# In a mixture-of-experts loop, SyncE issues an expert's gate and up weight loads ahead of its wait for the previous expert's landing

## The reference

```python
def moe(h, p):                        # 64 experts, top 8, 1152 tokens, fp32
    ...
    order = jnp.argsort(flat_e)       # assignments sorted by expert, padded to blocks of 128
    ...
    def expert_block(args):
        xb, e = args                  # 128 x 1024, the block's expert
        return (jax.nn.silu(xb @ p["w_exp_gate"][e]) * (xb @ p["w_exp_up"][e])) @ p["w_exp_down"][e]
    ...
    shared = (jax.nn.silu(x @ p["w_sh_gate"]) * (x @ p["w_sh_up"])) @ p["w_sh_down"]
    return (routed + shared)
```

## Time and profile before

| | before |
|---|---|
| median of 3 runs | 1864.94 us (1858.88 to 1868.56) |
| the profiled execution | 1868.01 us, of which the span of the instructions is 1866.2 us |
| granted TensorE clock, mean over the span | 0.967 |
| PE busy | 1712.8 us (92%) |
| DVE, ACT, POOL busy | 929.8, 845.4, 766.8 us |
| data moved | 389.75 MB, mean 209 GB/s |
| routed part | about 745 to 1800 us, 104 blocks |

### The profile page before, as it was taken

The page is one execution under the profiler, slowest core; times in us unless marked ns, Lnnn a source line. Parts: engine busy times, 40 slices in busy tenths (PEclk is TensorE's granted clock), DMA queues, the critical chain, the costliest instruction groups (busy, mean ns, idle before and its releaser), DMA issues.

```text
span 1866.2 us, 32108 instructions
## 1 busy us (share of the span) xinstructions
PE 1712.8 (92%) x8570; PEld 1331.5 (71%) x8571; DVE 929.8 (50%) x1442; ACT 845.4 (45%) x950; POOL 766.8 (41%) x445
## 2 busy tenths in 40 slices
PE   6899999999899778999989989999999989999845
PEld 2677788888455656888877877888878767887621
DVE  7432210177478843564463555334644654465529
ACT  2320012441133512675565666445765765566622
POOL 3230000400004552565555556535665556646530
PEclk9999999998999888999999999999999999999978
DMA  8515521023442533697788889866987788778666
GB/s 343 179 55 179 171 91 37 15 91 122 171 170 91 195 88 138 227 336 233 216 309 260 251 295 332 245 164 187 330 302 223 258 289 286 223 251 281 230 226 265
DMA packets 102447, 389.75 MB, mean 209 GB/s; under 512 B 21916, under 2 KB 38553, under 8 KB 74624
## 3 DMA queue, kind: packets, MB, share of 16 engines
q1 hardware_dynamic: 62576, 289.25, 41.9%
q0 software_dynamic: 37232, 90.42, 19.2%
q10 hardware_dynamic: 2592, 9.44, 1.8%
HBM read 339.94 MB, written 84.72 MB: 228 GB/s over the span
## 4 chain that ended last, share of the span: by engine, by line
PE 62%; DMA 13%; DVE 8%; issue 6%; ACT 5%; POOL 3%; ACTq 2%; SPq 1%; POOLq 0%; DVEq 0%
PE ps L856 32%; PE ps L2001 12%; DMA arena<-hx_dram,arena 5%; DMA raw<-w_exp_up 4%; PE ps L911 4%; PE ps L2142 4%; POOL d_split L594 2%; DMA acc_dram<-arena 2%; PE ps L1924 2%; ACT d_split L658 1%; PE ps L2132 1%; PE ps L1974 1%; ACTq L440 1%; PE ps L888 1%; PE ps L2097 1%
## 5 line engine op out<-in xcount | busy, mean ns | idle before, releaser
L856 PE MATMUL ps<-gu_split,xT 128*128 (+1 forms) x2712 | 641.7, 392 | 6.6 <-issue 6.2
L856 PEld LDWEIGHTS ps<-gu_split,xT 128*128 128x128 f32 x2712 | 510.9, 189 | 119.0 <-issue 13.5
L856 PE MATMUL ps<-d_split,hTe 128*128 (+1 forms) x1356 | 351.1, 409 | 37.6 <-ACT arena L734 35.5
L594 POOL TENSOR_TENSOR d_split<-raw,d_split (+1 forms) x65 | 299.4, 4606 | 196.4 <-ACT d_split L658 195.8
L987 DVE TENSOR_TENSOR gu_split<-raw,gu_split (+1 forms) x130 | 294.6, 2308 | 141.0 <-ACT gu_split L653 137.3
L856 PEld LDWEIGHTS ps<-d_split,hTe 128*128 128x128 f32 x1356 | 254.7, 194 | 93.9 <-issue 43.8
L653 ACT ACTIVATE gu_split<-raw (+1 forms) x130 | 241.8, 1908 | 70.5 <-SPq L496 48.0
L613 POOL DMA_INDIRECT arena<-hx_dram,arena x108 | 139.8, 1295 | 189.1 <-DVE arena L1157 154.8
L622 POOL DMA_INDIRECT acc_dram<-arena x104 | 175.1, 1684 | 92.5 <-DVE arena L1162 58.2
L1151 DVE TENSOR_TENSOR arena<-ps,arena 128x256 f32<-128x256 f32 x113 | 70.5, 624 | 276.8 <-ACT arena L740 273.3
L1141 DVE TENSOR_TENSOR xT<-ps,xT 128x1024 fp32r<-128x1024 f32 x115 | 140.8, 1224 | 106.4 <-ACT xT L712 98.2
(11 more groups left out here) (284 smaller groups left out, 1436.8 us busy)
## 6 DMA issues: line engine op xcount, KB each, us to landing
raw<-w_exp_gate SPq DMA_DIRECT2D x64, 1024.0 KB
raw<-w_exp_up SPq DMA_DIRECT2D x64, 1024.0 KB
raw<-w_exp_down SPq DMA_DIRECT2D x64, 1024.0 KB
arena<-w_ada SPq DMA_DIRECT2D x16, 1024.0 KB, 4.9
arena<-x_dram SPq DMA_DIRECT2D x18, 512.0 KB, 10.4
arena<-acc_dram SPq DMA_DIRECT2D x18, 512.0 KB, 11.2
arena<-ada_halves SPq DMA_DIRECT2D x4, 2048.0 KB, 24.3
w_raw<-w_in SPq DMA_DIRECT2D x16, 512.0 KB, 4.9
```

The source lines that it names most:

```text
L594: tt(d_split(q, 1), raw_d(q), d_split(q, 0).bitcast(F32), ALU.subtract).then_inc(d_low, 1)
L856: last = mm(dst, lhs(a, j), rhs(b, j), start=(t == 0), stop=(t == len(terms) - 1))
```

## The change

In SP's loop, `publish_gu` of expert x-1 moves from ahead of the wait for x-2's slot to behind the two issues for expert x. Nothing else is touched; the number of instructions stays the same on all engines.

```diff
@@ -536,9 +536,9 @@
                 for q in range(2):
 
                     x = 2 * m + 1 + q
-                    publish_gu(q, m + 1)
                     sp.wait_ge(gu_low, x - 1)
                     load_gate_up(sp, 1 - q, row("gate", x - 1), row("up", x - 1))
+                    publish_gu(q, m + 1)
                     sp.wait_ge(d_low, x - 2)
                     load_down(sp, q, row("down", x - 2))
                     publish_d(1 - q, m + q)
```

## The result

The changed kernel takes 1876.25 us (median of 9 runs, 1868.49 to 1879.74), the kernel before beside it 1863.85 us (9 runs, 1857.98 to 1870.66). The ratio is 1.0070 with a 95% interval of 1.0052 to 1.0087: slower by 13 us, with 10 to 16 as bounds. The forecast was 1874 us, 9 us or 0.5% above, so it lies just under that.

What follows compares the result with a forecast made beforehand. Expert matmuls fill most of the chain; slow stretches are bound by a ring through ACT, POOL and SP. Lengthening it gives +9.8 us, sooner loads -1, so about +9 us on the 1864.94 median: 1874 us, range 1862 to 1884.

Steps and rivals of the forecast that it cites:

- Where SP stands in the chain: SP matters only in slow stretches of one-block experts, about 11.96 us per block against 9.26 where PE is full.
- four entries with 0.88 or 0.89 us: Time from SP's down issue to ACT's gate copy, read as the landing not being late there.
- third place: Four ring periods from 1475.43 to 1526.30 us, 50.87 together; forecast to lose 5.0 us.
- last place: Three ring periods from 1721.41 to 1759.73 us, 38.32 together; entry unchanged, forecast to lose 1.6 us.
- The ring: Loop of ACT's down copy, POOL's down split, SP's down issue and signal, ACT's gate copy; 12.54 us becomes 13.68.
- four places: Where one-block experts follow one another, from 956.90, 1089.59, 1475.43 and 1721.41 us; losses +1.5, +1.7, +5.0, +1.6, sum +9.8 us.
- The price of a signal, 1.14 us: Delay of SP's signal in the ring: 0.29 set-up, 0.80 two issues, 0.05 more set-up; bounds 0.80 and 1.3.
- The sum by place: Entry delay plus lengthened periods, new minus old, added over the ring's four places: +9.8 us.
- What the change gives back, -1 us: Loads starting sooner share less transfer time with gathers: 0 to one us at each place, -4 at most, -1 taken.
- Outside the ring nothing: Where PE is busy throughout, the later signal needs 1.45 us of 2.28 available, so it costs nothing.
- fourth rival: Margin outside the ring fails: about 13 places lose up to 1 us each, +10 to +20 us; chance 0.12.
- The rule on issue time: Skill page's rule would put the moved issues at nothing, sum -4 us; the forecast charged 0.80 us per signal instead.

Runs made afterwards that it cites:

- late signal alone: Against the kernel before, SP notes the landing ahead of the loads as before; only its signal to ACT moves behind the two issues; 1.0102, +19 us.
- SP out of POOL's wait: ACT issues and awaits the down loads instead of SP; against the kernel before, 0.9886 and 0.9884 in the changed order, 1.0006 in the old order.
- half dose: Against the kernel before, the signal to ACT stands between the gate issue and the up issue; 1.0063 and, run again, 1.0035.

## Why the prediction was right, point by point

- **Where SP stands in the chain.** Right, though of the "four entries with 0.88 or 0.89 us" one lies inside the third place; the entry of the last place had 2.05, as the sum has it. The ring closes only where one-block experts follow one another, the four places are the same before and after, and PE's full stretches kept 9.3 us per block. The late signal alone brings the whole loss, and with SP out of POOL's wait the swap gains instead: the ring's part in the loss is shown.
- **The price of a signal, 1.14 us.** Right: 1.99 - 0.89 = 1.10 us in the chain; the half dose gave 13.23 us per period for 13.2. Its terms were each a little off: the first issue comes 0.18 us later than the signal did, not 0.29, and the issues take 0.86 us (1499.41 + 0.43 - 1498.98), not 0.80.
- **The sum by place.** 13.68 us per period was forecast, 13.72 at the third place was measured. By the starts of silu, from the step ahead of a place to the last step of it, the third place lost 5.2 us (forecast 5.0), the second 1.7 (1.7), the last 1.4 (1.6), the first 0.7 (1.5), since an earlier step there was late by 0.8 us before and not after. Together 9.0 us of the 10.4 in the routed part. One reading behind it was wrong. What stands above 12.54 us in the old periods was taken for late landings, 0.71 us at the third place. But SP has no wait for a landing there in the kernel before. Its periods alternate, 12.99, 12.54, 12.78 and 12.56 us, and so do those of the changed kernel, 13.82, 13.65, 13.79 and 13.62, which has next to no late landings. Every second expert SP also goes round its loop (line 535): from its down issue to its gate issue the changed kernel takes 1.00 us at 1484.30 and 0.72 at 1498.26. So part of the 0.71 us stayed and wasn't swallowed, and the four periods grew by 4.01 us instead of 3.85.
- **What the change gives back, -1 us.** Mis-sized. The late signal alone costs 19 us, the change 10 to 13; by the routed parts 4 to 10 us lie between them, at or past the -4 that I had set as the bound. And the cost side was mis-sized as well: 9.8 us was the lengthening at the ring's places alone, while the late signal alone adds 17.6 us to the routed part. Steps behind the ring's last period are longer too: the nine steps from the one ahead of the third place take 109.1 us, against 101.4 in the kernel before and 107.7 and 107.9 in the change, while the place alone is worth 5. As both kernels have this, it explains only 1 us of the difference between them; the rest is spread over the routed part. The two gathers in the chain behind that place took 13.15 and 12.99 us with the late signal and 11.24 and 11.17 in the kernel before on chip 13 (rows below). That sooner loads get out of the way of those gathers would fit, but the changed kernel's first one there took 12.86 us on chip 13 and 12.25 on chip 7, it rests on single profiles, and it wasn't tried by itself: this stays open. The two errors cancelled in part: 9.8 - 1 came near the measured 12.4 us by luck as well as by the ring. The rows, late signal alone first, then the kernel before:

```profile
1528.77 13.15 DMA arena<-hx_dram,arena
...
1587.44 12.99 DMA arena<-hx_dram,arena
```

```profile
1511.13 11.24 DMA arena<-hx_dram,arena
...
1569.51 11.17 DMA arena<-hx_dram,arena
```

- **Outside the ring nothing.** Right but for one place. There are 2.25 us of room as before. Of ACT's 15 waits for the signal 14 are at the ring's places, where ACT waited before too; the one that is new stands alone:

```profile
1306.02 3.72 ACT L653 ACTIVATE gu_split<-raw  x2 [1.31 <-SPq L496]
```

  Before, this copy started at 1310.76 with no wait noted, in a step that lay 6 us later in the trace. By the silu of the steps from 1290 to 1400 us the changed kernel loses about 2 us there in its first profile, and 1 or less in the other two. That is a delay of the kind of the fourth rival, at one place instead of 13.
- **The rule on issue time.** "Small relative to the DMA" (the Trainium skill, "DMA: Bandwidth & Descriptors", "Issuing engines are not separate DMA queues") holds for the transfer and misleads here: 0.8 us of issuing ahead of a signal cost 1.0 to 1.1 us per period. The same page's advice to issue early and wait late ("Rules for kernel authors") is borne out only where SP had nothing else to stand behind: +10 us with the ring, -22 us without it, of which 10 to 15 are in the routed part, on the runs above.

The forecast gave 0.51 to "no change that can be measured" and 0.41 to "slower". Slower it was, at 0.55 to 0.7% in all three comparisons, so the more likely of its two cases didn't come.

## What to carry to other kernels

A queue engine that both issues transfers and passes on their landings is a link between compute engines. Ask of each of its signals not only what it waits for but what stands ahead of it: an issue of 0.8 us that hides behind a 12 us transfer cost its full length in the loop that passed through the signal. And before moving a wait, look for the other wait on the same queue that sets the pace; with that one gone (here by letting the consumer issue and await its own load) the same move changed from a loss of 0.6% to a gain of 1.2%.

## What the runs showed of the hardware that was not expected

- The same kernel took 1863.85 us in the first comparison and 1838.5 to 1841.7 on the three chips of the experiments. In the profiles most of the difference lies ahead of the routed part, which starts at 753 us in the one and at 726 us in the other (kernel before, one profile each). PE is busy 47.01 of the 60 us behind 640 us in the first, at a mean granted clock of 0.89, and all 46 us behind 634 us at 1.00 in the other. Why isn't known; the mean periods of the ring at the third place agree within 0.02 us.
